# A first stage that loads its own input in parts, rotary tables made inside it, and weight blocks prepared two ahead

## The reference, cut to what matters

```python
def first_block(x, p, positions, ...):
    cos, sin = rope_tables(positions)
    h = x
    for i in range(2):
        h = layer_norm(ALPHA * h + 0.5 * swiglu(h, ffa_w_in[i], ffa_w_out[i]), ...)
        mix = hybrid_mixer(h, cos, sin, mix_w_in[i], ..., mix_w_o[i])
        h = layer_norm(ALPHA * h + mix, ...)
        h = layer_norm(ALPHA * h + 0.5 * swiglu(h, ffb_w_in[i], ffb_w_out[i]), ...)
        h = h + sigmoid(h @ ple_w_gate[i]) * (p[i] @ ple_w_proj[i])
    return h
# second block: a vector c gives shifts, scales and gates (silu(c) @ w_ada + b_ada);
# then swiglu, a mixer (sparse attention and a recurrence), swiglu, each modulated
def rope_tables(positions):
    ang = positions[..., None] * inv            # inv: 16 frequencies
    return cos(ang), sin(ang)
```

## Time and profile before

| | |
|---|---|
| median of 3 runs | 3728.72 us (3724.77 to 3733.86) |
| the profiled execution: its own time | 3735.12 us |
| its span, first to last instruction | 3733.3 us |
| PE busy | 3504.9 us, 94% of the span |
| DVE busy | 1759.6 us (47%) |
| ACT busy | 1222.7 us (33%) |
| mean granted PE clock | 0.973 of full speed |

### The profile page before, as it was taken

One profiled execution on the slowest core, in us unless ns is written; L12 is line 12 of the kernel. 1 busy time (PEld: TensorE's weight loads), 2 busy tenths in 40 slices (PEclk: granted clock), 3 DMA queues, 4 the chain that ended last, 5 costly groups with the idle time before them and its releaser, 6 DMA issues. The chain is left out here.

```text
span 3733.3 us, 46940 instructions
## 1 busy us (share of the span) xinstructions
PE 3504.9 (94%) x19692; PEld 2745.3 (74%) x19692; DVE 1759.6 (47%) x2177; ACT 1222.7 (33%) x1826; POOL 448.1 (12%) x367
## 2 busy tenths in 40 slices
PE   7999898899999999998988899998999989789998
PEld 5888676776888778886757678875788856558886
DVE  5542375456642466324744565324433248553322
ACT  2222334333222332224351332224322253543221
POOL 0002112440002000030115300030000100310001
PEclk9999999999999999999999999999999989899999
DMA  4333221013432244321200144321322212113331
GB/s 162 135 121 99 63 67 43 2 47 113 141 126 89 73 136 141 113 85 63 68 25 3 52 137 145 108 85 64 124 96 97 83 64 71 37 62 96 96 102 62
DMA packets 88011, 326.59 MB, mean 87 GB/s; under 512 B 12624, under 2 KB 12624, under 8 KB 87544
## 3 DMA queue, kind: packets, MB, share of 16 engines
q1 hardware_dynamic: 87800, 323.57, 26.2%
HBM read 321.15 MB, written 4.74 MB: 87 GB/s over the span
## 5 line engine op out<-in xcount | busy, mean ns | idle before, releaser
L227 DVE TENSOR_TENSOR w_low<-w_raw,w_high 128x1024 fp32r<-128x1024 f32 (+1 forms) x481 | 634.6, 1320 | 950.9 <-ACT w_high L219 949.8
L219 ACT ACTIVATE w_high<-w_raw 128x1024 fp32r<-128x1024 f32 (+1 forms) x481 | 536.1, 1115 | 587.1 <-PE ffa_ps L245 192.9
L243 PE MATMUL ffa_ps<-ffa_x_high,w_high 128*128 128x512 f32 x704 | 283.4, 403 | 32.5 <-DVE ffa_x_low L305 29.0
L243 PE MATMUL b_f_ps<-b_f_x_high,w_high 128*128 128x512 f32 x704 | 280.5, 398 | 12.7 <-DVE b_f_x_low L443 12.7
L244 PE MATMUL ffa_ps<-ffa_x_low,w_high 128*128 128x512 f32 x704 | 281.5, 400 | 0.0
L245 PE MATMUL ffa_ps<-ffa_x_high,w_low 128*128 128x512 f32 x704 | 280.7, 399 | 0.0
L244 PE MATMUL b_f_ps<-b_f_x_low,w_high 128*128 128x512 f32 x704 | 279.6, 397 | 0.0
L245 PE MATMUL b_f_ps<-b_f_x_high,w_low 128*128 128x512 f32 x704 | 279.4, 397 | 0.0
L243 PE MATMUL mix_proj_ps<-mix_x_high,w_high 128*128 128x512 f32 x416 | 171.4, 412 | 20.0 <-DVE mix_x_low L383 14.6
L243 PEld LDWEIGHTS ffa_ps<-ffa_x_high,w_high 128*128 128x128 f32 x704 | 134.0, 190 | 66.3 <-DVE w_low L227 24.0
L243 PEld LDWEIGHTS b_f_ps<-b_f_x_high,w_high 128*128 128x128 f32 x704 | 133.6, 190 | 47.5 <-issue 13.4
(11 more groups left out here) (550 smaller groups left out, 7101.0 us busy)
## 6 DMA issues: line engine op xcount, KB each, us to landing
w_raw<-in_ffa_in SPq DMA_DIRECT2D x88, 512.0 KB, 3.6
w_raw<-in_ffb_in SPq DMA_DIRECT2D x88, 512.0 KB, 3.6
w_raw<-in_ffn_in SPq DMA_DIRECT2D x88, 512.0 KB, 3.5
w_raw<-in_mix_in SPq DMA_DIRECT2D x77, 512.0 KB, 3.5
w_raw<-in_ffa_out SPq DMA_DIRECT2D x32, 704.0 KB, 4.1
w_raw<-in_ffb_out SPq DMA_DIRECT2D x32, 704.0 KB, 4.1
w_raw<-in_ffn_out SPq DMA_DIRECT2D x32, 704.0 KB, 4.0
ffa_ada_raw<-in_w_ada SPq DMA_DIRECT2D x36, 512.0 KB, 4.7
```

What stands on the lines that cost most here:

```text
L219: act.activation(self.high[:, self.place(n, 0, kt)], self.raw[:, n % SLOTS, :kt * P], ACT.Copy).then_inc(self.rounded, 1)
L227: dve.tensor_tensor(self.low[:, whole], self.raw[:, n % SLOTS, :kt * P], self.high[:, whole].bitcast(F32), ALU.subtract).then_inc(self.spl ...
L243: pe.matmul(out, w_high, x_high[:, k0 + k, :], start=start and place == 0, stop=False)
```

## The change

Five edits.

1. The stages `rope` and `silu` are gone. A new class `Opening`, given to the first feed forward only, does their work inside it: SP loads x in four parts of 512 KB, alternating with weight blocks 0 to 2, then the other tensors; ACT waits for each part where it rounds it; the tables are made by DVE in steps 47 to 49 and by ACT in step 50 (the second half).
2. In all feed forwards ACT and DVE prepare block n+2 instead of n+1 in the first half (`far`).
3. The rounding of the next stage's block 2 behind the last ACT instruction of a feed forward and of `out_proj` is dropped; the next stage does it after its fourth chunk, in the call that was there before.
4. `mixer_proj`: block n+2 in step n, and block 3 as soon as block 0 is used.
5. `second_proj`: the same.

```diff
-def split_high(act, rounded, x_high, x, chunks, beside=nothing):
+def split_high(act, rounded, x_high, x, chunks, beside=nothing, landed=()):
     for k in range(chunks):
+        if landed:
+            act.wait_ge(landed[k // 2], 16)
         act.activation(x_high[:, k, :], x[:, k, :], ACT.Copy).then_inc(rounded, 1)
...
@@ feed_forward
+    far = lambda n: max(n + 1, min(n + 2, IN_BLOCKS - 1))
...
+                if opening:
+                    opening.sync(sp, ws, first)
                 ws.load_upto(sp, first + SLOTS - 1)
...
+                if opening:
+                    opening.scalar_silu(act)
...
                 for n in range(blocks):
-                    ws.round_upto(act, first + n + 1)
+                    ws.round_upto(act, first + far(n))
...
+                    if opening and n == IN_BLOCKS + 6:
+                        opening.scalar_tables(act)
                 finish.scalar(act, lambda: ws.round_upto(act, first + blocks + 1))
-                ws.round_upto(act, first + blocks + 2)
...
-                        ws.split_upto(dve, first + n + 1)
+                        ws.split_upto(dve, first + far(n))
...
+                    if opening and n == 0:
+                        dve.wait_ge(opening.silu_done, 1)
...
+                    if opening and n == IN_BLOCKS + 3:
+                        opening.vector_angle(dve)
+                    if opening and n in (IN_BLOCKS + 4, IN_BLOCKS + 5):
+                        opening.vector_table(dve, n - IN_BLOCKS - 4)
...
@@ out_proj
-                ws.round_upto(act, first + KD + 2)
@@ mixer_proj; second_proj has the same three edits
                 for n in range(M1_BLOCKS):
-                    ws.round_upto(act, first + n + 1)
+                    ws.round_upto(act, first + n + 2)
...
                     act.wait_ge(ws.used, first + n + 1)
+                    if n == 0:
+                        ws.round_upto(act, first + FIRST)
...
-                    ws.split_upto(dve, first + n + 1)
+                    ws.split_upto(dve, first + max(n + 2, FIRST))
...
+class Opening:
+    def sync(self, sp, ws, first):
+        dst, src = self.x
+        for j in range(self.PARTS):
+            part = slice(2 * j, 2 * j + 2)
+            if j < 3:
+                ws.load_upto(sp, first + j)
+            sp.dma_start(dst[:, part, :], src[:, part, :]).then_inc(self.x_landed[j], 16)
+        sp.dma_start(*self.c_silu).then_inc(self.c_landed, 16)
+        sp.dma_start(*self.consts).then_inc(self.consts_landed, 16)
+        for dst, src in self.rest:
+            sp.dma_start(dst, src).then_inc(self.rest_landed, 16)
+    def scalar_tables(self, act):
+        for n, table in enumerate(self.tables):
+            act.wait_ge(self.reduced, n + 1)
+            act.activation(table, self.left[:, n, :], ACT.Sin).then_inc(self.tabled, 1)
+        act.preload_act_table_set(EXP_LN)
```

More of the change, by code:

```diff
@@ L326, with __init__ @@
     names = ["x_rounded", "x_ready"]
-    def __init__(self, x):
-        self.x = x
+    def __init__(self, x, opening=None):
+        self.x, self.opening = x, opening
     def signals(self, rounded, ready):
@@ L334, in scalar @@
     def scalar(self, act, x_high, beside=nothing):
-        split_high(act, self.rounded, x_high, self.x, KD, beside)
+        landed = self.opening.x_landed if self.opening else ()
+        split_high(act, self.rounded, x_high, self.x, KD, beside, landed)
     def vector(self, dve, x_high, x_low, beside=nothing):
@@ L462, with feed_forward @@
 IN_BLOCKS, OUT_BLOCKS = 2 * KF, 2 * KD
-def feed_forward(nc, ws, name, halves, finish, norm, small=(), modulation=None, ahead=None):
+def feed_forward(nc, ws, name, halves, finish, norm, small=(), modulation=None, ahead=None, opening=None):
     n_ps = 4
@@ L519, in _ @@
                         ahead.sync(sp)
+                    if opening and n == IN_BLOCKS:
+                        sp.wait_ge(ws.used, first + IN_BLOCKS)
+                        opening.sync_places(sp)
+                if opening:
+                    opening.sync_end(sp)
                 if small:
@@ L589, in _ @@
                 multiply_first(pe, ws, first, [ps[j][:, :] for j in range(FIRST)], x_high, x_low, halves.ready)
+                if opening:
+                    pe.wait_ge(opening.consts_landed, 16)
                 if modulation:
@@ L1956, in two_pi_parts @@
     return parts
[L1959 to L2000, removed]
@@ L3084, in build @@
             m.cos, m.sin = sb(first, "cos", [P, S]), sb(first, "sin", [P, S])
[L3085 to L3095, removed]
-                        act.activation(c_silu[:, :], c_silu[:, :], ACT.Silu).then_inc(silu_done, 1)
+            opening = Opening((h, t["x"]), (c_silu[:, :], t["c"]), (squares[:, :], t["squares"]),
+                              [(mod[:, :], t["b_ada"]), (gains[:, :, :], t["gains"])],
+                              (t["positions"].broadcast_to([P, S]), t["freq"]), (m.sin[:, :], m.cos[:, :]))
             layers = [{k: v[layer] for k, v in t.items() if k in LAYERED} for layer in range(DEPTH)]
@@ L3100, in build @@
                 with ExitStack() as own:
-                    first_layer(nc, ws, h, m, const, layers[layer], own, mod, c_silu, layer, norm)
+                    first_layer(nc, ws, h, m, const, layers[layer], own, mod, c_silu, layer, norm, None if layer else opening)
         second_block(nc, ws, h, mod, gains, const, t, norm, out)
@@ L3126, in second_blocks, with first_layer @@
     return feed_forward_of("ffn1") + at("mix2_in", M2_BLOCKS, KD) + at("mix2_out", KD, KD) + feed_forward_of("ffn2")
-def first_layer(nc, ws, h, m, const, t, ctx, mod, c_silu, layer, norm):
+def first_layer(nc, ws, h, m, const, t, ctx, mod, c_silu, layer, norm, opening):
     sb = lambda c, n, s: c.enter_context(nc.sbuf_tensor(f"{n}{layer}", s, F32))
@@ L3142, in first_layer @@
     normed = [NormHalves(h, norm, ln[:, 2 * k, :], ln[:, 2 * k + 1, :]) for k in range(3)]
-    feed_forward(nc, ws, f"ffa{layer}", SplitHalves(h), feed_forward_norm(h, norm, const, normed[0]), norm, params, modulation[0])
+    feed_forward(nc, ws, f"ffa{layer}", SplitHalves(h, opening), feed_forward_norm(h, norm, const, normed[0]), norm, params, modulation[0],
+                 opening=opening)
     with ExitStack() as mixer:
```

53 lines of the change are left out of this document (51 added, 2 removed).

## The result

The changed kernel takes 3692.39 us (median of 4 runs, 3686.91 to 3693.92), the kernel before 3731.29 (4 runs, 3724.77 to 3736.44, three of them known at the prediction): ratio 0.9894, 95% interval 0.9874 to 0.9914. The forecast was 3685.0 in a range of 3677 to 3701. The profiled executions differ by 3735.12 - 3693.34 = 41.8 us, the medians by 38.9; the sum of the prediction was 43.9.

A forecast was written before the change was run, and what follows sets the result against it. PE, busy 94% of the span, was taken as the bound, with only its idle time and slow clock to win. Gains of 18.5, 0.8, 7.6, 6.4 and 10.6 sum to 43.9 us, giving 3685 us, range 3677 to 3701.

The forecast's parts named there:

- Opening, 18.5: First feed forward: weights and x loaded first, PE starts at 8.1, block 4 ends at 41.1 instead of 59.59; 18.5 us gained.
- the 2.5 and 1.4 ascribed to two ahead: First feed forward: block 4's wait of 2.5 us and 1.4 of half clock behind it go through preparing two ahead.
- x's parts flow together: Opening: parts land 1.4 us apart; the rival, 3.9 us each one after another, gives 3691 us, chance 0.08.
- Tables for nothing: First feed forward's second half: making the tables there costs PE nothing; without that cover the opening gains 14 us.
- Feed forwards, 0.8: Three other modulated feed forwards: block 4's waits of 0.9 and twice 1.05 become 0.7 before block 3; 0.8 us gained.
- Boundaries, 7.6: Eight stage boundaries: without ACT's last rounding the barrier comes 0.95 us earlier at each; 7.6 us gained.
- Mixer, 6.4: Mixer projections of both layers: block 3's waits, 5.4 us, go, and 1.0 of half clock; 6.4 us gained.
- Projections, 10.6: Second block's projections (`b_proj`): waits for weights shrink by 4.3, 2.3 and 1.4 us, half clock by 2.6; 10.6 us gained.
- the block that inherits a stall: `b_proj`: block 4 might inherit block 3's wait, its split falling behind both convolutions; forecast no wait, no slack.
- The clock takes back: Rival: a slow-clock stretch elsewhere takes back what the waits give; 3690 us, chance 0.10.
- Two ahead gives nothing: Rival: waits for `w_low` only move on by a block; opening and boundaries alone stay, 3706.5 us, chance 0.09.
- Slower: Rival: rounding ahead of Silu and the bank's copy delays every product, up to 3962 us; chance 0.03.

The follow-up runs named there:

- Trial 1: Kernel before with only the new opening (x in four parts between weight blocks, tables made later), blocks still prepared one ahead: 3719.00 us, ratio 0.9966.
- trial 5: Changed kernel with x in one DMA of 2 MB between weight blocks 0 and 1, instead of four of 512 KB: 3694.72 us, 0.9904 of the kernel before.
- trial 6: Changed kernel with the DVE instructions of each rotary table issued twice: 3698.70 us, 0.9915 of the kernel before.
- trial 3: Kernel before with only `mixer_proj` and `second_proj` preparing two blocks ahead: 3721.13 us, ratio 0.9972.
- trial 4: Kernel before with only the feed forwards preparing block n+2 instead of n+1: 3728.40 us, ratio 0.9997.
- trial 9: Changed kernel with the sum of modulation column 0 ahead of block 3's split on DVE: 3692.55 us, 0.9895 of the kernel before.
- trial 11: Changed kernel plus x's chunks first, recurrence's DVE begin earlier, column 0's sum first and `ple` two ahead: 3678.39 us, 0.9858 of the kernel before.
- trial 2: Kernel before with only the rounding of the next stage's block 2 behind the last ACT instruction dropped: 3723.88 us, ratio 0.9980.
- trial 7: Changed kernel with weight blocks 1 and 2 loaded behind x's second and third parts, prepared behind chunks 2 and 3: 3690.22 us, 0.9900 of the kernel before.

## Why the prediction was right, and where it was off

The mechanism held, and the range held the time. By its steps:

- *Opening, 18.5.* It gave 17.3. First matmul 8.26 (8.1 forecast), second chunk 11.27 (10.8), ten slow matmuls at 0.43 each, as taken in the sum (0.235 and 0.2 more), column wait 0.91 (0.7), block 3 at 30.76 (29.9), block 4's Silu at 43.37, of which 1.05 is the rounding that now stands ahead of it. The term was mis-sized by 1.2, 0.9 of it up to the start of block 3. Trial 1 shows a flaw that the total hides: the 2.5 and 1.4 ascribed to two ahead would have shrunk by themselves.
- *x's parts flow together.* Right: 1.45 apart (1.4 forecast), and trial 5 prices them at 3.0. That rival is out.
- *Tables for nothing.* Right; trial 6 shows the cover: 8.9 more of DVE work (4.45 for each table) made PE wait 2.64, so about 6.3 us over these two blocks was left.
- *Feed forwards, 0.8.* In the three other modulated ones 1.4, read as what is left of `ffb` and `ffa` in the table above when the boundaries are taken off (1.0 + 2.0 less 0.33, 0.33 and 0.95).
- *Boundaries, 7.6.* Six at 0.95 and two at 0.33: 6.4. The step that failed is "the barrier comes 0.95 earlier" at `ffb`, where PE is next in line after 0.34.
- *Mixer, 6.4.* 7.1, two waits of 2.68 and the clock behind them.
- *Projections, 10.6.* 9.3. Waits of 4.3, 2.5 and 1.4 went down to 0.3, but the move bared a wait of 2.27 for `b_v`, and the one for `b_proj_keys_relu` at the search grew from 3.2 to 3.6. I had named the block that inherits a stall, and it did wait only 0.3; I had not followed the other product that ACT makes for PE there.
- *The rest of the miss.* Of the 7.4 between 3685.0 and 3692.4 the sum makes 2.1 (43.9 against 41.8). The five terms missed by 0.6 to 1.3 each, three one way and two the other, so that the sum came this close owes something to luck. 2.6 is the median of before, 3728.7 of three runs then and 3731.3 with the fourth, of 3736.44. 2.9 is that the profiled execution of the changed kernel lies only 1.0 above its median, that of before 3.8 above its own. The forecast was rounded up by 0.2, which comes off.
- *The clock takes back.* Not settled by the pair. The stretches at half clock behind three waits are gone from the changed kernel's trace, others came at the starts of stages, and trials 1 to 4 gave less in their medians (30.9 in sum) than outside (44.5); the four intervals together are wide enough for the 38.9.
- *Two ahead gives nothing*: out for the projections, by trial 3; for the feed forwards trial 4 shows 3.0 us in the first one, and its median, 3728.40, shows nothing. *Slower*: out by the same two.

## What to carry to other kernels

When the last arrival at a barrier or a bank is made earlier, the gain ends at the second to last: read when every engine arrives, not only the one that you move. When a stall goes, follow every queue that crossed it in its cover; here a 128x4 instruction behind four convolutions cost 2.3 us of PE once nothing hid it. At a start that is bound by DMA, issue in the order of need down to the smallest consumer: the 512 KB that DVE wanted first stood behind 2.5 MB that were wanted later.

## What the runs showed of the hardware

The attention and delta rule of the two mixers hold the same instructions in all fourteen profiled executions, and took from 362.6 to 379.3 us in them. The busy times of DVE, ACT and POOL hardly move; the granted clock does. Windows (stretch, length, busy us of PE, PEld, DVE, ACT, POOL, then PEclk, DMA, GB/s) over the attention of the second layer in trial 9 and trial 11:

```profile
1869.83:1941.66 71.83, 60.20 (x274) 37.78 (x274) 34.03 (x70) 38.94 (x99) 15.98 (x16) 0.83 0.03 10
```

```profile
1858.28:1922.17 63.89, 50.76 (x274) 32.55 (x274) 35.71 (x70) 38.72 (x99) 15.90 (x16) 0.97 0.04 11
```

and over the delta rule of the first layer in trial 9 and trial 2:

```profile
657.49:778.14 120.65, 106.81 (x2824) 96.10 (x2825) 57.95 (x118) 25.82 (x48) 50.85 (x45) 0.91 0.02 5
```

```profile
674.57:788.06 113.49, 100.19 (x2824) 91.77 (x2825) 57.43 (x118) 25.81 (x48) 50.82 (x45) 0.97 0.02 6
```

Between a granted clock of 0.83 and one of 0.97 lie 8 of these 72 us. In the five executions of trial 7, one kernel, the time went from 3687.26 at a mean granted clock of 0.976 to 3700.99 at 0.972. I see no edit upstream that moves these stretches one way; that they carry most of the spread of the medians, because PE waits often and shortly in them, is likely and not shown. That is why a gain of 2 to 3 us is read from the stages whose length repeats to 0.1 us (the projections of the mixers took 188.6 in each layer of all ten executions with the changed loops) and not from one median. The number of slow matmuls at the start of a kernel differs from run to run, says the Trainium skill (TensorE: Matmul & The Clock Gate, Part 1). These windows agree (0.83 and 0.97, 0.91 and 0.97), though they lie in the middle of the program and each pair comes from two kernels with the same instructions in that stretch.
